# Last two expert pairs placed by matrix products instead of a scatter, with token rows loaded and added beside the last pair

## Chip, cores and metric

One of the eight cores of a Trainium2 chip runs the whole program in one launch. The metric is the device time of that program in microseconds (us); less is better. All data are 32-bit floats.

## What is computed

Two transformer blocks on 512 token rows of width 1024. The change touches the last stage only, a mixture of experts, and the normalisation behind it. Cut to what matters (NE = 32 experts, two of them chosen per token, hidden width 256):

```python
for e in range(N_EXPERTS):
    he = silu(xt @ w_gate[e]) * (xt @ w_up[e])
    y = y + combine[:, e:e + 1] * (he @ w_down[e])
x = x + y
out = rms_norm(x) * final_norm
```

`combine` is zero except for the two experts that the router chose for the token, and holds their weights there. So 1024 (token, expert) products have to be made, weighted, and added to 512 rows.

## The kernel before

The engines run five instruction streams written out by hand, tied by semaphores: TensorE (PE), VectorE (DVE), ScalarE (ACT), GpSimd (POOL) and SyncE (SP). Each stream is strictly in order, so a wait in one holds up all that stands behind it.

**The expert stage.** A tile holds 128 rows: 64 slots for one expert and 64 for another. 24 such tiles ("pairs", `NP = 24`) are worked through in a fixed order: 16 main pairs (experts 2m and 2m+1 for m = 0 to 15) and 8 for experts with more than 64 rows (`OVER_AT`). Pair 22 holds main pair 14 (experts 28 and 29), pair 23 main pair 15 (experts 30 and 31). For pair n:

- POOL gathers the token rows of the slots from DRAM by an indirect DMA (L741); slots with no token have an index out of bounds and move nothing.
- PE turns the tile (`turn_tile`, L2118 to L2124, 8 transposes into PSUM banks 4 and 5); DVE copies it out (`tile_turned`, L1585).
- PE makes gate and up (`gate_up`, L2126, L2134: 16 matmuls, two at a time on the two halves of the array's columns) into PSUM bank n % 2; ACT applies silu (`half_tile`, L1121), DVE multiplies (`product`, L1599).
- PE turns the hidden rows (`turn_hidden`, L2143), ACT copies them (`copies`, L1125), PE makes down (`down`, L2155) into PSUM banks 2 and 3.
- ACT copies bank 2 and DVE bank 3 to the row buffer YO[n % 3] (L1131, L1605), and POOL scatters the 128 rows to the DRAM array `pair_rows` (`y_d`, L745) at (choice, token).

PE takes the pairs so that its gate/up for n + 1 stands ahead of the hidden turn and down of n (L2162 to L2168). SP loads the expert weights (4 MB of gate and up, 2 MB of down for a main pair) as their buffers come free (L572 to L579); the weights of overflow pairs come by indirect DMA on POOL (L747 to L764).

**Routing** is computed ahead of the stage by DVE (L1508 to L1583): slot indices (SLOT, L1575), then the two weights of each token (WGT, L1579 to L1582); `v_wr` reaches 2 with the last of them. POOL starts the gathers at `v_sl` (L767); PE starts at the first gathered tile.

**The end of the kernel.** SP waits until PE has done all gate/up and until *all* 24 scatters have landed (L581 to L583), then loads the pair rows of the four token tiles, 8 loads of 512 KB (L587). DVE adds weight times row to X, 8 instructions (L1623). ACT sums squares (L1142), POOL makes the inverse root (L611, L613 through `root`), DVE scales by it and by the norm's weight (L1629, L1630), and ACT issues the four stores of 512 KB (L1145).

Of the kernel before, what the change touches and what calls it, by code (L numbers as in the profile page):

```python
# [159 lines left out]

def tile_order(i):

    return ORDER.get(i, tuple(range(TILES[i])))
# [9 lines left out]
def build(nc, a, out):  # L173
    with ExitStack() as ctx:
# [104 lines left out]
        YO = [RM[:, 4096:5120], RM[:, 5120:6144], WUKV[:, :]]  # L279
        HE = [RM[:, 6144 + 256 * n:6400 + 256 * n] for n in range(2)]  # L280
# [122 lines left out]

        d_g = [sem(f"pairs_loaded{t}") for t in range(4)]
# [84 lines left out]
        def _(sp):  # L489
# [102 lines left out]
        def _(g):  # L592
# [141 lines left out]

            wgr, wur, wdr = (a[f"w_expert_{s}_2"][0].rearrange("e (p k) c -> (e p) (k c)", p=P) for s in ("gate", "up", "down"))
# [7 lines left out]
            def scatter(n):  # L743
                rows = row_at(ap=SLOT[:, 24 + column(n):25 + column(n)], axis=0)
                g.indirect_dma_start(y_d, rows, YO[n % 3], None, bounds_check=TOPK * T_X - 1, oob_is_err=False).then_inc(m_st[n % 3], 16)  # L745

# [25 lines left out]
            gather(4)  # L772
            over_gate_up(3)
            for n in range(NP + 1):
# [17 lines left out]
        def _(act):  # L792
# [334 lines left out]
            def rows(n):  # L1127
                act.wait_ge(m_dn, 2 * n + 1)
                if n >= 3:
                    act.wait_ge(m_st[n % 3], 16 * (n // 3))  # L1130
                A(YO[n % 3][:, 0:512], PS[:, 2, :], ACT.Copy).then_inc(m_ya, 1)  # L1131

            half_tile(0)
            for n in range(NP):
                if n + 1 < NP:
                    half_tile(n + 1)
                copies(n)
                rows(n)

            for t in range(4):  # L1140
                act.wait_ge(v_g, 2 * t + 2)
                A(XN[:, t, :], X[:, 2 + t, :], ACT.Square, scale=D ** -0.5, accum_out=ss[:, t:t + 1]).then_inc(a_fm, 1)  # L1142
            for t in range(4):
                act.wait_ge(v_fn, t + 1)
                act.dma_start(out[0].rearrange("(t p) d -> p t d", p=P)[:, t, :], X[:, 2 + t, :]).then_inc(d_out, 16)  # L1145
# [3 lines left out]
        def _(v):  # L1149
# [432 lines left out]
            v.tensor_tensor(WGT[:, :, 1:2], WGT[:, :, 0:1], tiles(EXPS, [1, 1], off=10), ALU.mult).then_inc(v_wr, 1)  # L1582
# [18 lines left out]
            def down_rows(n):  # L1601
                v.wait_ge(m_dn, 2 * n + 2)
                if n >= 3:
                    v.wait_ge(m_st[n % 3], 16 * (n // 3))
# [3 lines left out]
            tile_turned(1)  # L1608
            product(0)
# [7 lines left out]
            j = 0  # L1617
            for t in range(4):
                v.wait_ge(d_g[t], 32)
                for k in range(2):  # L1620
                    if k == 1:
                        v.wait_ge(v_g, j)
                    v.scalar_tensor_tensor(X[:, 2 + t, :], YP[:, 2 * t + k, :], WGT[:, t, k:k + 1], X[:, 2 + t, :], ALU.mult,  # L1623
                                           ALU.add).then_inc(v_g, 1)
                    j += 1
            v.wait_ge(d_fw, 16)
            for t in range(4):
# [6 lines left out]
        def _(pe):  # L1634
# [481 lines left out]
            pe.wait_ge(v_sl, 1)  # L2116

# [8 lines left out]
            def gate_up(n):  # L2126
# [5 lines left out]
                for k in range(8):  # L2132
# [3 lines left out]
                last.then_inc(m_gu, 1)  # L2136
# [90 lines left out]
```

## Time and profile before

| | |
|---|---|
| median of 3 runs | 1624.77 us (1624.53 to 1625.59) |
| the profiled execution | 1624.51 us |
| its span | 1622.7 us (so 1.8 us lie outside the span) |
| PE busy | 1502.9 us, 93% of the span |
| DVE, ACT, POOL busy | 522.3, 449.6, 331.1 us |
| chain that ended last, by engine | PE 88%, DMA 3%, ACT 3%, DVE 3% |
| mean granted clock | 0.973 |

The busy shares say that PE is nearly always at work; the chain says that PE is also what the end of the kernel goes back to. But neither says anything of one stage, so the end of the kernel has to be read from its own rows: instructions in order of time, the chain's last pieces, and the packets of each DMA queue in short windows. A DMA queue's row gives the packets, the MB and the time its packets took as a share of 16 DMA engines in the window asked for.

### The profile page before, as it was taken

How to read it: one execution, taken by the hardware profiler on the slowest of the kernel's cores; microseconds unless marked ns; L12 is line 12 of the kernel's file. 1: busy time of each engine (PE TensorE's matmuls, PEld its weight loads, DVE VectorE, ACT ScalarE, POOL GpSimd, SP SyncE). 2: the span in 40 equal slices, each digit the busy share in tenths (PEclk: the TensorE clock that was granted, in tenths of full speed). 3: DMA queues.
4: the chain of work that ended last, by engine and by line, in shares of the span. 5: the costliest groups of instructions: out<-in, count | busy, mean ns of one | idle time of the engine just before them, and what ended most of it. 6: DMA issues, size and time to landing. Idle time of an engine off the chain costs nothing.

```text
span 1622.7 us, 17325 instructions
## 1 busy us (share of the span) xinstructions
PE 1502.9 (93%) x6765; PEld 785.3 (48%) x6765; DVE 522.3 (32%) x1124; ACT 449.6 (28%) x881; POOL 331.1 (20%) x357
## 2 busy tenths in 40 slices
PE   5998989999999989999999899999999499999992
PEld 2676544455675444455675444455455333333330
DVE  1073310656433210666432211122143412111214
ACT  2234322222763241233762110232232101101101
POOL 1010000453000110555000000004422134323312
PEclk9999999999999999999999999999999699999996
DMA  9654113230110212120100123110500779999994
GB/s 353 239 212 170 53 64 144 78 119 37 50 58 1 94 52 78 53 83 21 55 1 1 52 104 104 52 44 29 193 1 27 275 265 414 369 412 398 402 409 177
DMA packets 85128, 232.98 MB, mean 144 GB/s; under 512 B 17026, under 2 KB 24968, under 8 KB 70841
## 3 DMA queue, kind: packets, MB, share of 16 engines
q1 hardware_dynamic: 69426, 201.93, 33.0%
q0 software_dynamic: 13824, 24.16, 4.1%
q10 hardware_dynamic: 1798, 5.80, 0.9%
q8 instruction: 54, 0.88, 0.2%
q14 instruction: 26, 0.21, 0.0%
HBM read 266.42 MB, written 16.80 MB: 175 GB/s over the span
## 4 chain that ended last, share of the span: by engine, by line
PE 88%; DMA 3%; ACT 3%; DVE 3%; issue 2%; POOL 0%; SPq 0%; DVEq 0%; POOLq 0%; ACTq 0%
PE PS L1719 19%; PE PS L2134 10%; PE PS L1887 9%; PE PS L1950 7%; PE PS L2155 5%; PE PS L1799 5%; PE PS L1698 4%; PE PS L1948 3%; PE PS L2043 3%; PE PS L1821 3%; PE PS L1809 2%; PE PS L1761 2%; PE PS L1985 1%; DMA RING<-in_w_mod_dram 1%; PE PS L2012 1%
## 5 line engine op out<-in xcount | busy, mean ns | idle before, releaser
L1719 PE MATMUL PS<-RH,RING 128*128 128x512 f32 (+1 forms) x864 | 315.9, 522 | 2.2 <-DMA RING<-in_w_in_dram 2.2
L1719 PEld LDWEIGHTS PS<-RH,RING 128*128 128x128 f32 x864 | 162.4, 190 | 146.9 <-issue 136.1
L1887 PE MATMUL PS<-RING,RY 128*128 128x512 f32 x320 | 139.5, 593 | 0.0
L2134 PE MATMUL PS<-RING,RM 128*64 128x512 f32 x384 | 116.7, 609 | 8.4 <-issue 5.6
L611 POOL TENSOR_SCALAR SMALL<-SMALL 128x1 f32<-128x1 f32 (+1 forms) x36 | 11.0, 306 | 537.7 <-ACT WS L833 266.1
L1249 DVE SCALAR_TENSOR_TENSOR RM<-RM,COL 128x512 f32<-128x512 f32 (+1 forms) x180 | 115.1, 707 | 0.2
L1950 PE MATMUL PS<-RH,RING 128*128 128x512 f32 x256 | 113.8, 593 | 0.0
L1290 DVE TENSOR_REDUCE SMALL<-PS 128x1 f32<-128x768 f32 (+1 forms) x80 | 68.0, 850 | 136.7 <-PE PS L1799 136.7
L1799 PE MATMUL PS<-RK,RH 96*128 96x256 f32 (+1 forms) x288 | 105.9, 487 | 1.1 <-ACT WS L976 0.7
L1887 PEld LDWEIGHTS PS<-RING,RY 128*128 128x128 f32 x320 | 60.1, 190 | 72.7 <-issue 72.7
L613 POOL TENSOR_TENSOR SMALL<-SMALL 128x1 f32<-128x1 f32 (+2 forms) x58 | 61.6, 1062 | 87.4 <-DVE SMALL L1223 84.4
L2134 PEld LDWEIGHTS PS<-RING,RM 128*64 128x64 f32 x384 | 37.4, 140 | 83.5 <-issue 80.1
L1950 PEld LDWEIGHTS PS<-RH,RING 128*128 128x128 f32 x256 | 47.2, 190 | 55.0 <-issue 55.0
L1121 ACT ACTIVATE RM<-PS 128x256 f32<-128x256 f32 x24 | 9.2, 385 | 221.7 <-PE PS L2134 221.7
L1799 PEld LDWEIGHTS PS<-RK,RH 96*128 96x128 f32 x288 | 49.9, 191 | 41.3 <-issue 39.4
L1698 PE MATMUL PS<-RING,RH 128*128 128x416 f32 (+1 forms) x192 | 62.9, 488 | 4.4 <-ACT RH L845 4.4
L976 ACT ACTIVATE WS<-PS,SMALL 128x768 f32<-128x768 f32 (+1 forms) x80 | 64.9, 812 | 3.0 <-DVE SMALL L1290 2.9
L1809 PE MATMUL PS<-CST,WS 128*128 128x128 f32 x416 | 59.4, 274 | 6.5 <-ACT WS L967 3.5
L1599 DVE TENSOR_TENSOR RM<-RM,PS 128x256 f32<-128x256 f32 x24 | 10.1, 421 | 160.3 <-ACT RM L1121 160.3
L2134 PE MATMUL PS<-RK,RM 128*64 128x512 f32 x128 | 58.6, 612 | 0.0
L1809 PEld LDWEIGHTS PS<-CST,WS 128*128 128x128 f32 x416 | 49.3, 141 | 18.4 <-issue 12.0
L1948 PE MATMUL PS<-RING,RH 128*128 128x512 f32 x128 | 56.4, 596 | 0.0
(336 smaller groups left out, 2251.0 us busy)
## 6 DMA issues: line engine op xcount, KB each, us to landing
RING<-in_w_in_dram SPq DMA_DIRECT2D x18, 2048.0 KB, 8.6
RING<-in_w_mod_dram SPq DMA_DIRECT2D x12, 2048.0 KB, 9.2
RING<-in_w_expert_gate_dram SPq DMA_DIRECT2D x19, 1024.0 KB
RING<-in_w_expert_up_dram SPq DMA_DIRECT2D x19, 1024.0 KB
RING<-in_w_out_dram SPq DMA_DIRECT2D x8, 2048.0 KB, 8.2
RK<-in_w_expert_down_dram SPq DMA_DIRECT2D x8, 1024.0 KB
X<-in_w_expert_down_dram SPq DMA_DIRECT2D x8, 1024.0 KB
WS<-in_w_expert_down_dram SPq DMA_DIRECT2D x8, 1024.0 KB
```

Of the source, the lines that this page charges most:

```text
L976: A(PR[n % 2][:, 0:nk], src, ACT.Exp, bias=nmx[:, n % 4:n % 4 + 1], accum_out=DEN[:, q % 2, h:h + 1]).then_inc(a_e.sem, 1)
L1249: ins = v.scalar_tensor_tensor(acc, src, w, acc, ALU.mult, ALU.add)
L1290: v.tensor_reduce(nmx[:, n % 4:n % 4 + 1], free(PS[:, 2 * (n % 2), :], [1, nk]), AX, ALU.max, negate=True).then_inc(v_mx.sem, 1)
L1698: last = mm(o[:, 0:width], HT[:, k, t * P:(t + 1) * P], w[:, k, :], start=(k == 0), stop=(k == 7))
L1719: last = mm(o[:, 0:T], w[:, k, m * P:(m + 1) * P], HT[:, k, 0:T], start=(k == 0), stop=(k == 7))
L1799: last = mm(PS[:, 2 * (n % 2) + c0 // 512, 0:w], RHf[0:QK, h * 512 + q * P:h * 512 + (q + 1) * P], KT[0:QK, h, c0:c0 + w], start=True, sto ...
L1809: last = tr(PS[:, 4 + j // 4, (j % 4) * P:(j % 4 + 1) * P], PR[k % 2][:, j * P:(j + 1) * P], IDENT)
L1887: last = mm(PS[:, j % 2, :], YT[:, k, t * P:(t + 1) * P], w[:, k, :], start=(k == 0), stop=(k == 7))
L1948: last = mm(PS[:, w % 2, :], HT[:, k, tile], wt[:, k, :], start=(k == 0), stop=(k == 7))
L1950: last = mm(PS[:, w % 2, :], wt[:, k, tile], HT[:, k, :], start=(k == 0), stop=(k == 7))
L2134: last = mm(PS[64 * z:64 * z + 64, n % 2, :], XGT[n % 2][:, k, 64 * z:64 * z + 64], free(GU[n % 3][z], [2048, 2], [1, DE], off=DE * k), st ...
L2155: last = mm(PS[64 * z:64 * z + 64, 2 + c, :], HET[n % 2][:, j, 64 * z:64 * z + 64], DN[n % 2][z][:, 1024 * j + 512 * c:1024 * j + 512 * c ...
```

## The change

Pairs 22 and 23 are no longer scattered. Instead:

- **Routing.** Behind the weights, DVE builds for each of the two pairs a 128 x 512 matrix LAST[z] (token by slot, the token's weight where the slot holds it, else zero) with two multiplies and an add of 512 columns each, and three small operations. PE turns the two matrices (8 transposes) before the first tile, ACT copies them out (`LAST_T`). Slot indices of pairs 22 and 23 are clamped to 511, so that their gathers move all 128 rows.
- **Zero rows.** POOL clears YO[2] before the stage, and scatters it twice, to the places of pairs 22 and 23, behind gather 4.
- **PE's order at the end.** Gate/up of pair 23 is cut in two with hidden turn and down of pair 22 between; two placing products stand behind it, two ahead of down of pair 23, four behind it, and then eight for pair 23's rows. A placing product is 128 x 128 by 128 x 512; 16 of them fill the eight PSUM banks with the 512 x 1024 sums.
- **Pair rows beside the last pair.** SP now waits for the hidden product of pair 22 and for the scatters up to pair 21 only. DVE adds the pair rows of token tile 0 *ahead of* `product(23)`, tile 1 behind it, tiles 2 and 3 behind the copy of pair 23's rows.
- **Final stage.** DVE adds the placed rows from PSUM (1024 columns, one instruction a tile), and scaling by root and weight is one instruction instead of two; SP instead of ACT issues the stores.

```diff
+def stored(n, b):
+    return sum(k % 3 == b for k in range(min(n, NP - 2))) + (2 if b == 2 else 0)
+        LAST_T = [WPWf[:, 0:512], WUQf[:, 1024:1536]]
+        LAST, PART = [WS[:, 2048:2560], WS[:, 0:512]], WS[:, 2560:3072]
...
-            sp.wait_ge(m_gu, NP - 1)
+            sp.wait_ge(m_he, NP - 1)
             for b in range(3):
-                sp.wait_ge(m_st[b], 16 * (NP // 3))
+                sp.wait_ge(m_st[b], 16 * stored(NP - 1, b))
...
+            for t in range(4):
+                sp.wait_ge(v_fn, t + 1)
+                sp.dma_start(out[0].rearrange("(t p) d -> p t d", p=P)[:, t, :], X[:, 2 + t, :]).then_inc(d_out, 16)
...
+            g.wait_ge(p_pv2, 32)
+            link(g.memset(YO[2], 0.0))
...
+            def zero_last():
+                for n in (NP - 2, NP - 1):
+                    rows = row_at(ap=SLOT[:, 24 + column(n):25 + column(n)], axis=0)
+                    g.indirect_dma_start(y_d, rows, YO[2], None, ...).then_inc(m_st[2], 16)
...
             gather(4)
+            zero_last()
             over_gate_up(3)
-            for n in range(NP + 1):
+            for n in range(NP - 1):
...
+            act.wait_ge(p_la, 1)
+            for z in range(2):
+                last = A(LAST_T[z], PS[:, 6 + z, :], ACT.Copy)
+            last.then_inc(a_la, 1)
             half_tile(0)
             for n in range(NP):
-                if n + 1 < NP:
+                if n + 1 < NP - 1:
                     half_tile(n + 1)
                 copies(n)
                 rows(n)
+                if n == NP - 2:
+                    half_tile(NP - 1)
...
+            link(v.tensor_tensor(free(SCR, [4, 8], ...), free(ONEHOT, ...), free(FIRST, ...), ALU.mult))
+            link(v.tensor_tensor(free(SCR, [4, 8], ...), free(SCR, ...), free(WGT...), ALU.mult))
+            v.tensor_scalar(SLOT[:, 14:16], PS[:, 1, 270:272], float(NONE), float(T_X - 1), ALU.add, ALU.min)
+            for z in range(2):
+                for k, dst in enumerate((LAST[z], PART)):
+                    last = v.tensor_tensor(free(dst, [P, 4], [64, 2], [1, 64]), free(OHR, ...), free(SCR, ...), ALU.mult)
+                link(last)
+                last = v.tensor_tensor(LAST[z], LAST[z], PART, ALU.add)
...
+            last.then_inc(v_wr, 1)
             v.wait_ge(v_wr, 2)
...
             for n in range(NP):
-                if n + 1 < NP:
+                if n + 1 < NP - 1:
                     product(n + 1)
                 if n + 2 < NP:
                     tile_turned(n + 2)
+                if n == NP - 1:
+                    pair_sums(0)
+                    product(n)
+                    pair_sums(1)
                 down_rows(n)
...
+            pair_sums(2)
+            pair_sums(3)
+            last_sums(0)
+            last_sums(1)
             v.wait_ge(d_fw, 16)
-            for t in range(4):
-                v.wait_ge(g_fn, t + 1)
-                link(v.tensor_scalar(X[:, 2 + t, :], X[:, 2 + t, :], rs[:, t:t + 1], None, ALU.mult))
-                v.tensor_tensor(X[:, 2 + t, :], X[:, 2 + t, :], GB[:, :], ALU.mult).then_inc(v_fn, 1)
+            final_rows(0)
+            last_sums(2)
+            final_rows(1)
+            last_sums(3)
+            final_rows(2)
+            final_rows(3)
...
+            pe.wait_ge(v_wr, 2)
+            for z in range(2):
+                for t in range(4):
+                    last = tr(PS[:, 6 + z, t * P:(t + 1) * P], LAST[z][:, t * P:(t + 1) * P], IDENT)
+            last.then_inc(p_la, 1)
...
             def down(n):
...
+                if n == NP - 1:
+                    pe.wait_ge(a_la, 1)
+                    place(0, 3, 1)
+                    place(0, 0, 0)
...
+            def place(z, t, c):
+                return mm(PS[:, 2 * t + c, :], LAST_T[z][:, t * P:(t + 1) * P], YO[(NP - 2 + z) % 3][:, 512 * c:512 * c + 512],
+                          start=(z == 0), stop=(z == 1))
...
             for n in range(NP):
                 if n + 1 < NP:
-                    gate_up(n + 1)
+                    gate_up(n + 1, range(8) if n + 2 < NP else range(4))
                 turn_hidden(n)
                 if n + 2 < NP:
                     turn_tile(n + 2)
                 down(n)
+                if n + 2 == NP:
+                    gate_up(n + 1, range(4, 8))
+                    pe.wait_ge(m_ya, NP - 1)
+                    pe.wait_ge(m_yv, NP - 1)
+                    place(0, 2, 0)
+                    place(0, 2, 1)
+
+            pe.wait_ge(m_yv, NP)
+            place(0, 0, 1)
+            pe.wait_ge(m_ya, NP)
+            place(0, 1, 0)
+            place(0, 1, 1)
+            place(0, 3, 0)
+            for t in range(4):
+                place(1, t, 0)
+                place(1, t, 1).then_inc(p_fin, 1)
```

`pair_sums(t)` waits for the two loads of token tile t and runs the two weighted additions that stood at L1623; `last_sums(t)` waits for `p_fin` t + 1 and adds PSUM banks 2t and 2t + 1 to X; `final_rows(t)` waits for the root and does X times root times weight in one instruction.

## Rows read from the trace of the kernel before

**Rows 1.** The page: span, granted clock and DMA share in 40 slices.
```profile
span 1622.7 us, 17325 instructions
PEclk9999999999999999999999999999999699999996
DMA  9654113230110212120100123110500779999994
```

**Rows 2.** The chain that ended last, its last 47 us: start us, us, what.
```profile
1575.56 7.02 PE PS L2134 x32
...
1583.40 3.65 PE PS L2155 x16
1587.06 0.39 PE PS L2143 x2
...
1587.94 3.67 PE PS L2155 x16
...
1591.63 0.70 DVE WUKV L1605
...
1593.16 2.56 DMA pair_rows<-WUKV,SLOT
...
1595.81 0.33 SPq L587
...
1618.00 1.23 DVE X L1630
```

**Rows 3.** Groups by line and shape, 1575 to 1623 us: xcount | busy us, mean ns.
```profile
L1623 DVE SCALAR_TENSOR_TENSOR X<-RING,WGT,X 128x1024 f32<-128x1024 f32 x8 | 10.2, 1286 | 9.1 <-DMA RING<-pair_rows 8.9
...
L613 POOL TENSOR_TENSOR SMALL<-SMALL 128x1 f32<-128x1 f32 x4 | 5.6, 1390 | 0.3
L1630 DVE TENSOR_TENSOR X<-X,GB 128x1024 f32<-128x1024 f32 x4 | 4.9, 1226 | 0.1
...
L1142 ACT ACTIVATE RY<-X 128x1024 f32<-128x1024 f32 x4 | 4.2, 1058 | 17.6 <-DVE X L1623 17.6
...
L1142 ACT ACTIVATION_READ_ACCUMULATOR RY<-X 128x1 f32 x4 | 0.7, 186 | 0.0
```

**Rows 4.** Timeline: start us, us, engine, line, operation.
```profile
1199.06 3.60 PE L2043 MATMUL PS<-RING,WS 128*128 128x512 f32 x8
...
1571.19 0.42 DVE L1599 TENSOR_TENSOR RM<-RM,PS 128x256 f32<-128x256 f32 x1 [6.59 <-ACT RM L1121]
...
1577.13 0.98 POOL L745 DMA_INDIRECT pair_rows<-RM,SLOT x1 [10.72 <-DVE RM L1605]
...
1600.76 2.61 DVE L1623 SCALAR_TENSOR_TENSOR X<-RING,WGT,X 128x1024 f32<-128x1024 f32 x2 [8.44 <-DMA RING<-pair_rows]
```

**Rows 5.** DMA queues: 1577.1 to 1581, 1581 to 1586, 1588.5 to 1592.5, 1592.5 to 1596.1.
```profile
q1 hardware_dynamic: 197, 1.43, 94.8%
...
q0 software_dynamic: 144, 0.30, 15.5%
...
q0 software_dynamic: 144, 0.18, 12.1%
...
q0 software_dynamic: 144, 0.05, 5.0%
```

**Rows 6.** The chain around two restarts of PE at low clock.
```profile
1298.43 9.30 PE PS L2134 x32
...
1417.75 3.88 issue
1421.63 8.78 PE PS L2134 x32
```

**Rows 7.** Before the stage: a 512-column DVE operation, and the first gather on the chain.
```profile
1281.01 0.68 DVE L1558 TENSOR_TENSOR WS<-WS 128x512 f32<-128x512 f32 x1
...
1287.19 7.71 DMA RM<-normed_rows,SLOT
```

**Rows 8.** Window around gather 23: engines' busy us, clock, DMA share, GB/s.
```profile
1520.00:1530.00 10.00, 10.00 (x54) 3.88 (x52) 2.40 (x4) 1.34 (x3) 1.62 (x2) 1.00 0.97 369
```

More of the change, by code:

```diff
@@ L1581, in _ @@
             link(v.reciprocal(WGT[:, :, 0:1], total))
-            v.tensor_tensor(WGT[:, :, 1:2], WGT[:, :, 0:1], tiles(EXPS, [1, 1], off=10), ALU.mult).then_inc(v_wr, 1)
+            link(v.tensor_tensor(WGT[:, :, 1:2], WGT[:, :, 0:1], tiles(EXPS, [1, 1], off=10), ALU.mult))
+            link(v.tensor_tensor(free(SCR, [4, 8], [1, 4], off=16), free(ONEHOT, [32, 8], [1, 4], off=28), free(FIRST, [1, 8], [0, 4]), ALU.mult))
+            link(v.tensor_tensor(free(SCR, [4, 8], [1, 4], off=16), free(SCR, [4, 8], [1, 4], off=16),
+                                 free(WGT[:, :, :].rearrange("p t k -> p (t k)"), [1, 8], [0, 4]), ALU.mult))
+            v.tensor_scalar(SLOT[:, 14:16], PS[:, 1, 270:272], float(NONE), float(T_X - 1), ALU.add, ALU.min)
+            for z in range(2):
+                for k, dst in enumerate((LAST[z], PART)):
+                    last = v.tensor_tensor(free(dst, [P, 4], [64, 2], [1, 64]), free(OHR, [P, 4], [0, 2], [1, 64], off=64 * k),
+                                           free(SCR, [8, 4], [1, 2], [0, 64], off=16 + 4 * k + 2 * z), ALU.mult)
+                link(last)
+                last = v.tensor_tensor(LAST[z], LAST[z], PART, ALU.add)
+                if z == 0:
+                    link(last)
+            last.then_inc(v_wr, 1)
             v.wait_ge(v_wr, 2)
@@ L1608, in _, with pair_sums @@
             tile_turned(1)
+            def pair_sums(t):
+                v.wait_ge(d_g[t], 32)
+                xt = X[:, 2 + t, :]
+                for k in range(TOPK):
+                    link(v.scalar_tensor_tensor(xt, YP[:, 2 * t + k, :], WGT[:, t, k:k + 1], xt, ALU.mult, ALU.add))
             product(0)
             for n in range(NP):
-                if n + 1 < NP:
+                if n + 1 < NP - 1:
                     product(n + 1)
@@ L1614, in _, with last_sums, final_rows @@
                     tile_turned(n + 2)
+                if n == NP - 1:
+                    pair_sums(0)
+                    product(n)
+                    pair_sums(1)
                 down_rows(n)
[L1617 to L1625, printed above, removed]
-            v.wait_ge(d_fw, 16)
-            for t in range(4):
-                v.wait_ge(g_fn, t + 1)
-                link(v.tensor_scalar(X[:, 2 + t, :], X[:, 2 + t, :], rs[:, t:t + 1], None, ALU.mult))
-                v.tensor_tensor(X[:, 2 + t, :], X[:, 2 + t, :], GB[:, :], ALU.mult).then_inc(v_fn, 1)
+            def last_sums(t):
+                v.wait_ge(p_fin, t + 1)
+                v.tensor_tensor(X[:, 2 + t, :], X[:, 2 + t, :], free(PS[:, 2 * t, :], [1, D]), ALU.add).then_inc(v_g, 1)
+            def final_rows(t):
+                v.wait_ge(g_fn, t + 1)
+                v.scalar_tensor_tensor(X[:, 2 + t, :], X[:, 2 + t, :], rs[:, t:t + 1], GB[:, :], ALU.mult, ALU.mult).then_inc(v_fn, 1)
+            pair_sums(2)
+            pair_sums(3)
+            last_sums(0)
+            last_sums(1)
+            v.wait_ge(d_fw, 16)
+            final_rows(0)
[4 more added lines that the diff above has]
+            final_rows(3)
         @block.tensor
@@ L2124, in turn_tile, with gate_up @@
                 last.then_inc(m_xt, 1)
-            def gate_up(n):
+            def gate_up(n, ks=range(8)):
                 pe.wait_ge(m_xc, n + 1)
@@ L2131, in gate_up @@
                     pe.wait_ge(m_he, n - 1)
-                for k in range(8):
+                for k in ks:
                     for z in range(2):
@@ L2135, in gate_up @@
                                   free(GU[n % 3][z], [2048, 2], [1, DE], off=DE * k), start=(k == 0), stop=(k == 7))
-                last.then_inc(m_gu, 1)
+                if ks[-1] == 7:
+                    last.then_inc(m_gu, 1)
             def turn_hidden(n):
```

14 lines of the change are left out of this document (7 added, 7 removed).

## The prediction, made before the changed kernel was run

> **What bounds the kernel now.** I read the page first. PE works through nearly the whole span at the full clock, and the DMA engines stand at 0.9 or more through the second half of the expert stage [rows 1]. So two resources are near their limit there, and what lies behind the stage is neither. The chain's last pieces come next: gate/up of the last pair, two down products, DVE's copy, the last scatter, SP's loads, additions, final scaling [rows 2]. From the end of the last down (1587.94 + 3.67 = 1591.6) to the end of the span (1622.7) are 31.1 us with PE idle. Its price list: scatter 2.56; first load issued 1595.81, first addition 1600.76, so 4.95 to land a token tile's two loads [rows 2, 4]; eight additions of 1.29; the last DVE instruction ends at 1619.23, and 3.5 us of store and end follow [rows 2, 3]. The change takes the scatter, the loads and most additions out of these 31 us, and puts PE work in.
>
> **The loads' new start.** Loads now wait for scatter 21 only. It was issued at 1577.13 [rows 4], and it is tempting to let it land 2.56 us later, as the last one did. The queue rows say otherwise. From 1577.1 to 1581 only q1 (SP's weights) moved packets, 1.43 MB; all 144 packets of the scatter (q0) stand between 1581 and 1586 [rows 5]. The scatters of pairs 22 and 23, alone on the engines, were done inside the windows shown, some 2.5 us after their issue. So a scatter amid weight traffic took 8 to 9 us. What delays it, the down weights of pair 23 issued at about 1575.6, is still there. I take 1586.0 for SP's first load, 9.8 us earlier than before, and 1591.0 for tile 0's data.
>
> Here a rule speaks for the change. The Trainium skill (DMA: Bandwidth & Descriptors, Queues, rings and completion order) has each DMA engine alternate between the queues that have work, packet by packet; by that the scatter would share from its issue on and land near 1580 to 1582. The trace disagrees for the first 4 us after issue, in which q0 had no packet. What it would be worth is the third case below.
>
> **More bytes.** The clamped indices make gathers 22 and 23 move 256 rows. The two scatters moved 0.18 + 0.05 MB [rows 5], 56 rows of 4 KB, so 200 rows or 0.82 MB are new, 2.2 us at the 1.43 MB in 3.9 us of the full engines [rows 5]. They fall around 1514 to 1531, where the share dips to 0.97 for 10 us [rows 8]; the dip absorbs about half, and I push the queue's end, so the loads, by 1.1 us (bounds 0 and 2.2): data at 1592.1. Weights themselves have room: gate/up of pair 23 started right behind down, and of the 2.18 MB that q1 moved after 1577.1 some 2.1 are the down weights of pair 23 [rows 5], so those of pair 22 had landed by about 1577.3; they are now wanted at 1580.0, and 1.6 us are left.
>
> **PE up to the last product.** Half of pair 23's gate/up is 7.02 / 2 = 3.5, to 1579.1. Hidden turn to down is 1587.94 - 1587.06 = 0.88, now with nothing beside it; down 3.65, to 1583.6; second half, to 1587.1 [rows 2]. A placing product is a 128 x 128 by 128 x 512 float matmul; four such in L2043 (eight rows of the trace) took 3.60, so 0.9 each [rows 4]. Two of them: PE is free at 1588.9.
>
> **The new wait.** Behind DVE's copy of pair 22's rows stands `pair_sums(0)`, *ahead* of `product(23)`. It waits for tile 0's data at 1592.1 and takes 2.61 [rows 4]; only then comes the product, 0.42 [rows 4], at 1595.2 with the hops. Queued behind that product are PE's whole remaining work and DVE's copy of the last rows. Before, it ran right behind silu. PE idles from 1588.9 to 1595.2, 6.3 us, which nothing covers.
>
> **What PE does then.** Turn and copy 0.88, two placing products 1.8, down 3.67, DVE's copy 0.7 and hops: 1602.3. Four placing products 3.6, and two for tile 0 of pair 23: the first signal of placed rows at 1607.7; the others follow 1.8 apart, the last at 1613.1. `pair_sums(1)` fits beside PE (its data land 3 us behind tile 0's), tiles 2 and 3 (5.2 us) fit between 1602.3 and 1607.7.
>
> **The tail.** Addition from PSUM 1.29 (priced as an addition of 1024 columns in SBUF); ACT 1.06 + 0.19; POOL's root about 1.3 with DVE mostly idle (the power alone 1.39 on average beside busy DVE); `final_rows` 1.29 instead of two instructions [rows 3]. By DVE's order: sum 0, square, root, final 0, sum 2, final 1, sum 3 = 1.29 + 1.25 + 1.3 + 4 x 1.29 = 9.0, to 1616.7; then square, root 1.7 and final 3, 4.3, to 1621.0. PE's last signal (1613.1) comes before DVE asks for it at 1615.4. Plus 3.5: the span would be 1624.5.
>
> **PE's clock.** After the wait of 3.88 us at 1417.75 the next gate/up took 8.78 instead of 7.02, and after the start of the stage 9.30 [rows 6]: the granted clock was at its lower level, 1.2 of 2.4 GHz, for some us, and 1.8 to 2.3 us were lost. An idle time of 6.3 us should do the same. I take 2.3, lower bound 0; upper bound: everything left at the lower clock, which adds 11.3 before the first signal and makes the last one late by another 3.1, 14.4 in all.
>
> **Edits that cost nothing.** Routing: six 512-column operations of 0.68 [rows 7] and three small ones, 4.7 us from 1286.9; eight transposes at twice 0.39 for each two, 3.1; that ends at 1294.7, and the first gather lands only at 1287.19 + 7.71 = 1294.9 [rows 7]. The cover is thin; if it goes, up to 1 us is lost. Zero rows: two issues of 0.98 and 0.3 between them put pair 3's indirect weight loads 2.6 us back, wanted 30 us later; their bytes fall where the DMA's slice shows 0.7 [rows 1]. The clearing of YO[2], about 1 us on POOL, lies some 15 us before anything needs it. ACT's copies of LAST_T end before its first silu. SP's stores wait behind nothing.
>
> **The sum.** 1624.5 + 2.3 = 1626.8 us of span against 1622.7; with 1.8 outside the span **1628.6 us** against 1624.51 of the profiled execution and the median 1624.77: slower by 0.24%. In two terms: pair 23's down starts 9.9 us later than before (1597.8 against 1587.94), and from its end 23.0 us are left to go instead of 31.1, so 1.8 are lost at the full clock and 2.3 by the clock. About 0.2% (3.2 us) is what a measurement of this kernel can tell from no change.
>
> **Rivals.**
> - *The clock holds or the gathers' extra bytes are absorbed.* All as above without the 2.3, or also without the 1.1: 1626.3 or 1625.2, no difference that can be measured. For it: the clock's price rests on two restarts only. Against: 6.3 us is longer than the 3.88 us after which the clock did fall.
> - *The scatter lands early (the other side).* Mechanism: scatter 21 shares the engines from its issue and lands by 1580 to 1582; the loads then stand in q1 right behind the down weights, whose last 0.75 MB ran after 1581 [rows 5], so tile 0's 1.05 MB land near 1586.5 instead of 1592.1. `pair_sums(0)` ends at 1589.1, PE waits under 1 us, no clock is lost: 1628.6 - 5.6 - 2.3 = 1620.7, faster by 0.25%. It decides if the loads start before about 1582. This is the rule of the skill's DMA page put into this kernel; against it stand the q0 packets after 1581.
> - *The clock stays low to the end.* PE works in pieces of 2 to 4 us with waits of 0.5 to 0.8 between them; if that isn't enough to raise it, 1628.6 - 2.3 + 14.4 = 1640.7, slower by 1%. Against: at the start of the stage it rose within one gate/up.
> - *The stage itself stalls.* The saturated queue already lets PE wait 3.88 us at 1417.75 [rows 6]; if the new bytes or POOL's delay lengthen such a wait by 2 to 3 us, 1631.
>
> **How the numbers follow.** Forecast (the wait, with one stretch of low clock) 0.50; clock holds or bytes absorbed 0.22; early scatter 0.12; clock low for long 0.09; stage stalls 0.07. The prices of the forecast are good to about 2 us each way, and the bound to "slower" lies at 1628.0, so some six tenths of it (0.30) count as slower, with 0.16 of the last two: slower 0.46. Of the early scatter 0.09 is faster, with 0.01 from errors elsewhere: faster 0.10. Same 0.44. The range leaves out about a tenth on each side: the early scatter's better half below, the long low clock above: 1621.5 to 1633.
>
> **What would show it.** Right: SP's first L587 load at 1585 to 1588; DVE idle till 1590 to 1593 ahead of two additions that stand before the last product; PE idle 5 to 7 us before the last hidden turn; the granted clock at 0.5 for some us behind it; the six or so products behind the last copy 0.9 each; final instruction near 1623. Wrong: loads issued by 1582, PE waiting under 2 us, the clock at 1.00 throughout, POOL's roots well off 1.3 us, an addition from PSUM that takes far more than 1.3 us, or PE starting pair 0 later than 1295.

## The result: slower by 0.3%, and the profile after

The changed kernel took 1631.15 us (median of 5 runs, 1628.77 to 1632.8) against 1624.77 (median of 5, 1623.07 to 1626.88): ratio 1.0031, 95% interval 1.0019 to 1.0042. (The ratio is the one on record; the quotient of the two medians is a little larger, 1.0039.) The forecast was 1628.6 us, +0.24%. The profiled run took 1631.15 us too, with a span of 1629.3.

The page after, for [rows 1]. Slice for slice the granted clock and the DMA share are nearly those of before. What changed isn't to be seen at this scale, and the closer views are needed:

```profile
span 1629.3 us, 17422 instructions
...
PEclk8999999999999999999999999999999699999997
DMA  9655114231110212120100122110500779999993
```

Two points are needed before the traces can be compared. First, the part ahead of the expert stage moves by itself from run to run: the instruction that forms SLOT started at 1286.01 in the trace of before, at 1288.69 after, and at 1290.15 and 1288.80 in two further traces that differ from before only in their last microseconds. Second, the stage itself kept its length: from that instruction to the end of pair 21's down there were 289.55 us before (1286.01 to 1575.56), 288.84 after (1288.69 to 1577.53), and between 288.9 and 291.1 in the traces of the experiments. So I count everything from the end of pair 21's down, and call that point E. From E to the end of the span: 47.1 us before, 51.8 after. That is +4.7, against +5.0 by the ratio.

The chain that ended last, after (start us, us, what), for [rows 2]:

```profile
1573.92 3.61 PE PS L2218 x16
...
1579.08 8.22 DMA pair_rows<-RM,SLOT
...
1587.36 0.33 SPq L596
...
1587.73 4.56 DMA RING<-pair_rows
...
1592.31 1.30 DVE X L1651
...
1594.95 0.43 DVE RM L1637
...
1595.42 0.70 PE PS L2202 x2
...
1596.59 3.78 PE PS L2223 x4
1600.37 4.09 PE PS L2218 x16
...
1604.54 0.70 DVE WUKV L1643
...
1605.28 5.43 PE PS L2223 x12
...
1610.81 1.23 DVE X L1667
...
1620.31 0.22 POOL SMALL L623
...
1621.22 1.28 DVE X L1671
```

Read it downwards. The scatter of pair 21 is issued 1.5 us behind E, takes 8.22 us, the second load of token tile 0 another 4.6, and two additions later DVE comes to the last product (L1637). PE's last turn (L2202) waits for it. Then one pass of placing products, the last down, DVE's copy, the placing products of the first tile, and an alternation of DVE, ACT and POOL to 1622.50.

How long PE waited is in the timeline (start us, us, engine, line, operation, in brackets the idle time before and what ended it):

```profile
1595.42 0.69 PE L2202 MATMUL PS<-CST,RM 128*128 128x128 f32 x2 [3.39 <-DVE RM L1637]
```

What its clock did is in the windows of 2 us around it (length, then PE, PEld, DVE, ACT and POOL busy, granted clock, DMA share, GB/s):

```profile
1594.00:1596.00 2.00, 0.57 (x2) 0.29 (x2) 1.33 (x2) 0.00 (x0) 0.00 (x0) 0.62 1.03 401
1596.00:1598.00 2.00, 1.53 (x3) 0.84 (x3) 1.65 (x2) 0.38 (x1) 0.00 (x0) 0.50 1.02 416
1598.00:1600.00 2.00, 2.00 (x3) 0.34 (x1) 0.92 (x1) 0.00 (x0) 0.00 (x0) 0.50 0.82 332
1600.00:1602.00 2.00, 2.00 (x7) 0.63 (x8) 0.00 (x0) 0.00 (x0) 0.00 (x0) 0.67 0.03 10
1602.00:1604.00 2.00, 2.00 (x12) 0.56 (x8) 0.00 (x0) 0.60 (x1) 0.00 (x0) 1.00 0.00 0
```

PE idled 3.39 us, its clock fell towards the end of that time (0.62 in the window 1594 to 1596) to 0.50 (1.2 of 2.4 GHz), and was back at 1.00 from 1602. That is the forecast's mechanism, with a shorter wait.

The surprise stands at the other end. The last DVE instruction ended 43.7 us behind E before (1619.23) and 45.0 after (1622.50): only 1.3 later. But from there to the end of the span it took 3.5 us before and **6.8 after**. SP's waits at the program's closing line, after, show why (engine, line, waited for: total us, times, longest):

```profile
SPq L180 <- PEq L180: 4.0, 1, 4.0
SPq L180 <- DMA out_dram<-X: 2.3, 1, 2.3
```

The queue instructions of that closing line, after (duration in ns: shortest/median/longest, then first and last start):

```profile
L180 POOLq EVENT_SEMAPHORE  x2: 17/17/17, 1629.2 to 1629.2; - x2
...
L180 POOLq DRAIN  x1: 8542/8542/8542, 1620.6 to 1620.6; - x1
```

The last store had landed at 1625.2; then SP waited 4.0 us more. The view puts that wait down to PE's queue, but PE's drain had ended long before (it began at 1608.0 and took 7.9). What ends at 1629.2 is POOL's closing DRAIN: 1620.6 + 8.54. POOL's last instruction, the power of the last root, ended at 1621.2, so the drain ends 8.0 us behind it. The same lines of the kernel before:

```profile
L174 POOLq EVENT_SEMAPHORE  x2: 17/17/17, 1622.5 to 1622.6; - x2
...
L174 POOLq DRAIN  x1: 8897/8897/8897, 1613.6 to 1613.6; - x1
...
L174 SPq COMPARE_BRANCH  x1: 38/38/38, 1621.9 to 1621.9; - x1
```

There too the span ended with POOL's drain (1613.6 + 8.9 = 1622.5, 8.0 behind the last root's end at 1614.54), but the stores had landed only 0.6 us earlier, so it passed for "store and end". Which engine issues the stores makes no difference here: ACT before, SP after, and the last store has landed 2.7 us behind the last DVE instruction in both (1619.23 to 1621.9, 1622.50 to 1625.2). The change moves the last root from 39.0 to 43.7 us behind E (1614.54 and 1621.19), and the end of the span follows it.

### The profile page after: what moved, and what is told of

Read it like the earlier page. It is cut to its first block, busy times and chain, and to the rows that moved or that the text cites. A ratio compares the mean times of both kernels' runs of the same rounds, so it can differ in the third digit from the quotient of the medians.

```text
span 1629.3 us, 17422 instructions
## 1 busy us (share of the span) xinstructions
PE 1526.4 (94%) x6805; PEld 795.8 (49%) x6805; DVE 528.8 (32%) x1133; ACT 450.6 (28%) x883; POOL 328.9 (20%) x358
## 4 chain that ended last, share of the span: by engine, by line
PE 89%; DMA 3%; ACT 3%; DVE 3%; issue 2%; POOL 0%; SPq 0%; POOLq 0%; DVEq 0%; ACTq 0%
PE PS L1772 19%; PE PS L2192 10%; PE PS L1940 8%; PE PS L2003 7%; PE PS L2218 5%; PE PS L1852 5%; PE PS L1751 4%; PE PS L2001 3%; PE PS L2096 3%; PE PS L1874 3%; PE PS L1862 3%; PE PS L1814 2%; PE PS L2038 1%; PE PS L2065 1%; PE PS L2181 1%
## 5 line engine op out<-in xcount | busy, mean ns | idle before, releaser
L625 POOL TENSOR_TENSOR SMALL<-SMALL 128x1 f32<-128x1 f32 (+2 forms) x58 | 58.3, 1005 | 87.3 <-DVE SMALL L1247 84.4
L1637 DVE TENSOR_TENSOR RM<-RM,PS 128x256 f32<-128x256 f32 x24 | 10.1, 421 | 153.6 <-ACT RM L1142 153.6
L2192 PE MATMUL PS<-RH,RM 128*64 128x512 f32 x128 | 56.4, 592 | 0.6 <-issue 0.6
```

The lines of the kernel that those rows point to most:

```text
L625: g.tensor_tensor(dst, src, HALF[:, 0:w], ALU.pow).then_inc(done, 1)
L2192: last = mm(PS[64 * z:64 * z + 64, n % 2, :], XGT[n % 2][:, k, 64 * z:64 * z + 64], free(GU[n % 3][z], [2048, 2], [1, DE], off=DE * k), st ...
```

## The experiments

Two theories were to be told apart. **The wait:** the loss comes from `pair_sums(0)` ahead of `product(23)`, through PE's idle time and its clock. **The end:** the span ends with POOL's drain, so the place of the last root counts. Rivals were the extra bytes of the gathers and the traffic around the scatter. For each run the table gives the ratio to the kernel before, as it ran in the same session as the experiment (medians 1625.75 to 1626.46 us there; the quotient of two medians can lie up to 0.0008 off the ratio), and from its trace the last DVE instruction's end behind E, the time from there to the end of the span, and both together. The times behind E are of one trace each; the kernel before and e10 and e3, which differ from it only behind the last scatter, have 43.7, 44.4 and 44.5 in the first column of times.

| kernel | ratio (95%) | last DVE behind E | to the end | sum |
|---|---|---|---|---|
| before | 1 | 43.7 | 3.5 | 47.1 |
| changed | 1.0031 (1.0019 to 1.0042) | 45.0 | 6.8 | 51.8 |
| e1 product first | 0.9996 (0.9986 to 1.0006) | 38.7 | 6.9 | 45.5 |
| e5 three extra products | 1.0022 (1.0014 to 1.0031) | 46.5 | 6.9 | 53.4 |
| e11 five extra products | 1.0015 (1.0006 to 1.0024) | 42.8 | 6.9 | 49.7 |
| e3 before, late POOL | 1.0041 (1.0027 to 1.0056) | 44.5 | 8.4 | 52.8 |
| e2 roots by Ln, Exp | 1.0045 (1.0029 to 1.0061) | 51.6 | 3.0 | 54.6 |
| e7 roots by Sqrt | 1.0000 (0.9990 to 1.0010) | 44.8 | 3.0 | 47.9 |
| e10 before, roots by Sqrt | 1.0002 (0.9993 to 1.0011) | 44.4 | 3.2 | 47.6 |
| e6 sums first | 1.0022 (1.0011 to 1.0033) | 45.4 | 6.9 | 52.3 |
| e4 no clamp | 1.0028 (1.0017 to 1.0039) | 45.8 | 6.8 | 52.6 |
| e8 down weights later | 1.0011 (1.0002 to 1.0019) | 43.2 | 6.8 | 50.0 |
| e9 = e1 + e7 | 0.9957 (0.9944 to 0.9971) | 38.7 | 3.1 | 41.8 |
| e12 = e1 + e7 + e8 | 0.9980 (0.9970 to 0.9991) | 41.9 | 3.0 | 44.9 |

### The wait and the clock

**e1**, the changed kernel with one line moved:

```diff
                 if n == NP - 1:
-                    pair_sums(0)
                     product(n)
+                    pair_sums(0)
                     pair_sums(1)
```

> The changed kernel with product(23) ahead of pair_sums(0) on DVE, nothing else. Theory (the new wait costs, by idle time and by low clock): in the changed kernel's trace PE was free at 1592.0 and got the product at 1595.4, then ran the turn, two placing products and down at 8.6 us instead of 5.9. With the product right behind silu PE has no idle time there and stays at the full clock, so the span falls by 3.4 + 2.7 = about 6 us, to about 1623 (device about 1625, level with the kernel before). Rival (the loads' additions only fill time that DVE would need anyway, so the work moves behind the last copy): DVE then has 5.2 us of additions between down and the placed rows, and the gain is 1 us or less.

Ratio 0.9996 and 45.5 us behind E: 6.3 less than the changed kernel (by the two ratios 5.7). The chain of e1 (start us, us, what) holds neither the scatter nor a load; up to the last down it is PE with ACT's short copies between:

```profile
1591.81 1.92 PE PS L2223 x4
1593.72 0.23 PE PS L2202 x2
...
1594.41 1.98 PE PS L2223 x4
1596.40 3.61 PE PS L2218 x16
```

PE goes from the placing products into the last turn without a gap. From the start of the turn to the end of down are 6.29 us, against 9.04 in the changed kernel (1595.42 to 1604.46). So of the 6.3 us, 2.7 are low clock and the remaining 3.6 are about the idle time of 3.39. The idle time is the larger part of what this order loses.

**e5** and **e11** keep the wait and try to take only the clock's part away, with products whose result is not used (in e11 the range is 5):

```diff
             def turn_hidden(n):
+                if n == NP - 1:
+                    pe.wait_ge(a_la, 1)
+                    for _ in range(3):
+                        mm(PS[:, 7, :], LAST_T[0][:, 0:P], YO[(NP - 2) % 3][:, 0:512], start=True, stop=True)
                 pe.wait_ge(m_he, n + 1)
```

> The changed kernel with three products of 128x128 by 128x512 put ahead of PE's wait for the last product; their result goes to PSUM bank 7 and is overwritten, so they add no value and take 2.6 us of the 3.4 us in which PE idles. Theory (the idle time lowers the clock, and that costs 2.7 us of its own: turn 0.70 instead of 0.39, two placing products 3.78 instead of 1.9, down 4.09 instead of 3.6): the clock stays at 1.00, the time from the start of the last hidden turn to the end of down falls from 9.0 to about 6.4 us, and the span from gate/up's end on by about 2.7. Rival (only the wait costs; the clock is made up for by DVE's additions behind it): the pieces shrink but the end moves less than 0.5 us.

e5 didn't settle it. In its trace tile 0's data came late (first addition at 1594.29, 7.0 us behind the first load instead of 5.0), three products (2.7 us) ended before that, PE was idle another 3.5 us ahead of its last turn at 1597.40, and the clock fell to 0.50 again (from 1599): turn to the end of down 8.2 us. The edit hadn't produced the condition that it was to test. Hence e11:

> As the run with three products in PE's wait, but five (4.3 us), since with three PE still idled 3.2 us (tile 0's rows came later in that run) and the clock fell to 0.5 all the same. Theory (low clock costs 2.7 us of its own): now PE doesn't idle, the clock stays at 1.00, the last turn starts at most 1 us later than the product allows, and turn to end of down takes 6.4 us instead of 9.0; in all 1.5 to 2.5 us less than the changed kernel behind the last product. Rival (the slow pieces have another reason than the idle time): they stay at 9.0.

Its chain (start us, us, what) shows the turn at once behind the product, and the work behind it at full speed; its windows read 1.00 in every stretch of 2 us from 1590 to 1602:

```profile
1594.20 0.45 PE PS L2206 x2
...
1595.11 1.98 PE PS L2227 x4
1597.09 3.61 PE PS L2222 x16
```

Turn to the end of down took 6.50 instead of 9.04, the wait for the product being unchanged. The clock's price is 2.5 us here. At the end of the span 2.1 us of it are left (51.8 to 49.7); by the ratios it is 1.0031 to 1.0015, some 2.6 us, with overlapping intervals.

### What ends the span

**e3** tests the drain on the kernel before, where nothing else moves:

```diff
                 root(rs[:, t:t + 1], ss[:, t:t + 1], g_fn)
+            g.wait_ge(v_fn, 4)
+            g.tensor_tensor(nmx[:, 0:1], HALF[:, 0:1], HALF[:, 0:1], ALU.mult)
```

> The kernel before with one tiny POOL multiply (128x1) that waits for the last rows of DVE (1619.2 in its trace). Theory (the end is POOL's last instruction plus 8.0 us): the span ends at about 1619.3 + 0.3 + 8.0 = 1627.6 instead of 1622.7, 5 us later. Rival (stores end the span): no change, since the multiply ends before the last store has landed.

One multiplication of 128 x 1 on POOL, of which nothing uses the result, made the kernel before 0.41% slower, 6.7 us. SP's wait at the closing line, in e3:

```profile
SPq L174 <- PEq L174: 5.6, 1, 5.6
```

And POOL's instruction of that line, in e3 (ns, first and last start):

```profile
L174 POOLq DRAIN  x1: 8145/8145/8145, 1623.6 to 1623.6; - x1
```

POOL's last instruction ended at 1623.8, the drain at 1631.75, the span at 1631.9. Again 8.0 us.

**e2** takes the last roots off POOL, to ACT:

```diff
-            for t in range(4):
-                g.wait_ge(a_fm, t + 1)
-                root(rs[:, t:t + 1], ss[:, t:t + 1], g_fn)
...
+            A(nmx[:, 0:1], epsc, ACT.Ln)
             for t in range(4):
                 act.wait_ge(v_g, t + 1)
-                A(XN[:, t, :], X[:, 2 + t, :], ACT.Square, scale=D ** -0.5, accum_out=ss[:, t:t + 1]).then_inc(a_fm, 1)
+                link(A(XN[:, t, :], X[:, 2 + t, :], ACT.Square, scale=D ** -0.5, accum_out=ss[:, t:t + 1]))
+                link(A(ss[:, t:t + 1], ss[:, t:t + 1], ACT.Ln, bias=epsc))
+                A(rs[:, t:t + 1], ss[:, t:t + 1], ACT.Exp, scale=-0.5).then_inc(g_fn, 1)
```

> The changed kernel with the four last inverse roots made by ACT (logarithm and exponential, about 0.6 us a root instead of 0.9 on POOL), so that POOL's last instruction is scatter 21. Theory (the end of the span is POOL's last instruction plus about 8.0 us, which its closing drain takes; the stores land 4 us before that in the changed kernel): without late POOL work the span ends at the landing of the last store plus under 1 us, some 3.5 us earlier, about 1625.5. Rival (stores end the span, as the prediction had it): no change, or 0.3 us each for the quicker roots, at most 1 us in all.

Half of it came: 3.0 us from the last DVE instruction to the end, so the drain is out of the way. But the last DVE instruction came 6.6 us later, so its trace ends 2.8 us later than the changed kernel's (54.6 behind E). The ratio, 1.0045, is higher too, with overlapping intervals. ACT's timeline gives the reason; its end, for the last tile:

```profile
1627.16 1.28 ACT L1168 ACT_TABLE_LOAD   x1
1628.45 0.29 ACT L1168 ACTIVATE SMALL<-SMALL 128x1 f32<-128x1 f32 x1
1628.77 1.28 ACT L1169 ACT_TABLE_LOAD   x1
1630.06 0.20 ACT L1169 ACTIVATE SMALL<-SMALL 128x1 f32<-128x1 f32 x1
```

Ln and Exp in turn each load a table of functions here, so a root costs 3.1 us. My edit carried a cost of its own. The Trainium skill (ScalarE: Activation LUTs, What ACT_TABLE_LOAD costs) gives about 1283 ns for a load, which the trace confirms at 1.28, and a drain of about 1380 ns more for every switch of set; of that the trace shows nothing, the loads stand directly between their neighbours.

**e7** avoids that: Square and Sqrt on ACT, the reciprocal on DVE (the removal on POOL as in e2):

```diff
+            A(nmx[:, 0:1], epsc, ACT.Sqrt)
             for t in range(4):
                 act.wait_ge(v_g, t + 1)
-                A(XN[:, t, :], X[:, 2 + t, :], ACT.Square, scale=D ** -0.5, accum_out=ss[:, t:t + 1]).then_inc(a_fm, 1)
+                link(A(XN[:, t, :], X[:, 2 + t, :], ACT.Square, scale=D ** -0.5, accum_out=ss[:, t:t + 1]))
+                A(ss[:, t:t + 1], ss[:, t:t + 1], ACT.Sqrt, bias=epsc).then_inc(g_fn, 1)
...
                 v.wait_ge(g_fn, t + 1)
+                link(v.reciprocal(rs[:, t:t + 1], ss[:, t:t + 1]))
```

> The changed kernel with the four last roots as a square root on ACT and a reciprocal on DVE, POOL with nothing behind scatter 21. In the run with logarithm and exponential each root loaded two function tables of 1.28 us, which ate the gain, but POOL's drain ended 40 us before the span. Theory: with one table the root takes about 0.3 us on ACT and 0.2 on DVE, nothing of POOL is late, and the span ends under 1 us behind the last store: 3.5 to 4.5 us earlier than the changed kernel. Rival (what ended the span there was something else that POOL only happened to cover): less than 1 us.

The closing line of e7, POOL's drain and SP's first instruction behind the stores (ns, first and last start):

```profile
L180 POOLq DRAIN  x1: 12851/12851/12851, 1579.9 to 1579.9; - x1
...
L180 SPq COMPARE_BRANCH  x1: 38/38/38, 1626.0 to 1626.0; - x1
```

The last DVE instruction ended 44.8 us behind E instead of 45.0, practically where it was, and the end came 3.0 us behind it instead of 6.8. POOL's drain now runs from 1579.9, beside the stage's end, and the span ends with the last store (1626.0). What differs is where and how the root is made, and DVE's own end hardly moved by it, so the 3.8 us between 6.8 and 3.0 are what the drain costs the changed kernel. **e10** puts the same roots into the kernel before:

> The kernel before with the same square-root form of the last roots, POOL with nothing behind its last scatter. Theory: there the drain ended only 0.6 us behind the last store's landing, so the gain is 0.5 to 1 us. Rival (POOL's roots cost the kernel before as much as the changed one): 4 us.

1.0002, no difference. That fits the 0.6 us by which the drain ended behind the stores in before, and shows that e7's gain isn't one of cheaper roots: before had next to nothing there to win, the changed kernel has.

**e6** tries to bring the last root forward by order alone, with `last_sums(2)` and `last_sums(3)` ahead of all `final_rows`:

```diff
             last_sums(1)
+            last_sums(2)
+            last_sums(3)
             v.wait_ge(d_fw, 16)
             final_rows(0)
-            last_sums(2)
             final_rows(1)
-            last_sums(3)
             final_rows(2)
```

> The changed kernel with all four last_sums ahead of the four final_rows on DVE. It brings the last square and POOL's last root forward (PE's last placed rows are there 2 us before DVE asks for them) while the last store stays where it is. Theory (POOL's last root plus 8.0 us ends the span): 1.5 to 2 us earlier than the changed kernel from the last placed rows on. Rival (the last store ends it): no change, 0.3 us at most.

No gain to be told (1.0022, 52.3 us). From the first addition from PSUM to the last square it took 6.3 us (1610.17 to 1616.51) instead of 8.3 (1610.81 to 1619.07), but the last root ran beside three `final_rows` on DVE. POOL's timeline, third and fourth root of e6:

```profile
1616.03 0.22 POOL L623 TENSOR_SCALAR SMALL<-SMALL 128x1 f32<-128x1 f32 x1 [0.84 <-ACT RY L1169]
1616.34 0.57 POOL L625 TENSOR_TENSOR SMALL<-SMALL 128x1 f32<-128x1 f32 x1
...
1617.74 1.20 POOL L623 TENSOR_SCALAR SMALL<-SMALL 128x1 f32<-128x1 f32 x1 [0.84 <-ACT RY L1169]
1619.03 1.46 POOL L625 TENSOR_TENSOR SMALL<-SMALL 128x1 f32<-128x1 f32 x1
```

0.79 us of work against 2.66, for the same two instructions. The Trainium skill (SBUF — State Buffer, Who interferes with whom) states that a DVE instruction with two inputs from SBUF contends with a POOL instruction that reads SBUF, for a shared pair of ports that is an exclusive lock. The trace agrees: `final_rows` has X and GB as such inputs, and beside it the times are stretched; beside the additions that read one input from PSUM the first three roots kept 0.22 and 0.57. What the order gives, the slow root takes back. So the run doesn't test an earlier root; its drain, too, ended 8.0 us behind the last root's end (1620.49 and 1628.4).

### The bytes and the scatter

**e4** leaves out the clamp of the indices of the last two gathers, so that their unused rows are not loaded:

```diff
-            v.tensor_scalar(SLOT[:, 14:16], PS[:, 1, 270:272], float(NONE), float(T_X - 1), ALU.add, ALU.min)
```

> The changed kernel without the clamp of slot indices 14 and 15, so gathers 22 and 23 move 56 rows instead of 256 (slots without a token keep older rows, whose weight in LAST is zero). Theory (the 0.82 MB push the queue's end by about 1.1 us): gate/up of pair 23 starts without the 0.6 us of waiting that the changed kernel shows, scatter 21 and so SP's loads come about 1 us earlier after gate/up of pair 23 has started, and the span shrinks by 1 us. Rival (the DMA's free time before 1531 takes the bytes): no difference.

The bytes are really gone: in the window 1530 to 1540 the DMA engines moved 345 GB/s at a share of 0.92, against 414 at 1.03 after, some 0.7 MB. The time is not: 1.0028, and the scatter landed 9.39 us behind its issue. The forecast's 1.1 us for the extra bytes isn't confirmed by anything.

**e8** holds the down weights of pair 23 (2.1 MB) back on SP until tile 0's two loads are issued:

```diff
             sp.wait_ge(m_dn, 2 * (NP - 2))
-            load_down(NP - 1)
...
                     sp.dma_start(YP[:, 2 * t + k, :], pairs[:, k, t, :]).then_inc(d_g[t], 16)
+                if t == 0:
+                    load_down(NP - 1)
```

> The changed kernel with the loads of pair 23's down weights behind the loads of token tile 0 on SP instead of ahead of the wait for scatter 21. Theory (the scatter is late because q1 holds 2.1 MB of weights issued 1.5 us before it): with only the rest of pair 22's weights in q1 the scatter lands 3 to 5 us after its issue instead of 8.2, tile 0's rows are there before 1588 on the changed kernel's clock, DVE adds them while PE is still at gate/up, PE's wait of 3.4 us and the low clock are gone, and the span falls by about 6 us, as with the product put first. Down weights of pair 23 still land before they are wanted. Rival (a scatter amid the stage takes some 8 us whatever q1 holds): landing after 8 us again, no gain.

Its chain (start us, us, what; the long "issue" is PE waiting for the down weights: its down product waits for nothing else that isn't long done):

```profile
1579.13 5.54 DMA pair_rows<-RM,SLOT
...
1585.17 4.46 DMA RING<-pair_rows
...
1593.64 1.98 issue
1595.62 3.52 PE PS L2223 x4
```

The scatter landed in 5.54 us instead of 8.22: against 8.1 to 9.4 in the traces with the weights in place, so they did delay it, by some 2.7. The DMA queues show where: in the changed kernel no packet of the scatter (q0) stands before 1583.0, 3.9 us behind its issue, while q1 held the engines at a share of 0.91 and then 1.01; in e8 the first ones stand 1.4 to 1.9 us behind the issue (66 of 144 between 1580.5 and 1581). But the weights are needed too: PE now waited 1.98 us for them ahead of its placing products, at low clock. The net was 1.8 us less than the changed kernel in the trace. The 5.54 are still twice the 2.56 of a scatter alone [rows 2], and not by a late start: alone, too, the first packets stood 1.4 to 1.8 us behind the issue (1593.16, and 123 of 144 between 1594.6 and 1595). What took longer is the spread of the packets, down to the last 8, which moved one by one between 1583 and 1584.7. Why was not tried.

### The best of them

**e9** is e1 and e7 together.

> The changed kernel with both mends: product(23) ahead of pair_sums(0), and the four last roots by a square root on ACT and a reciprocal on DVE. Theory (the two losses stand one behind the other: 6 us of wait and clock, 4 us of POOL's drain): 10 us less than the changed kernel, about 1620, so 0.3 to 0.4% faster than the kernel before. Rival (with the wait gone, DVE's own additions bind the tail, and quicker roots give little): 1624, level.

1620.84 us (median of 5 runs, 1619.1 to 1622.42) against 1626.46 for the kernel before in the same session, ratio 0.9957 (0.9944 to 0.9971): faster than both kernels. The parts add up: 6.3 by e1 and 3.9 by e7 make 10.2, and e9 is 10.0 us below the changed kernel (51.8 to 41.8). Its chain (start us, us, what):

```profile
1579.33 8.46 DMA pair_rows<-RM,SLOT
...
1590.43 9.79 DMA RING<-pair_rows
...
1600.24 1.30 DVE X L1650
...
1615.24 1.28 DVE X L1671
```

Now PE is off the chain: the last tile's loads land at 1600.22 and four additions follow. **e12** adds e8's later weights, to bring those loads forward:

> Product first, square-root roots, and the down weights of pair 23 behind the loads of tile 0. The down weights moved back made PE wait 2.0 us for them ahead of the last down, though the scatter landed 5.5 instead of 8.2 us after its issue. Theory (with the product first the rows' landing is no longer on the chain, so an early scatter gives nothing and late down weights cost their wait): 1 to 3 us slower than product first with square roots alone. Rival (tile 0's additions done earlier shorten DVE's tail): 1 us faster than that.

It was slower than e9 (0.9980 against 0.9957, the intervals just touching; 44.9 against 41.8 us behind E), though its scatter had landed within 5.0 us: PE reached the last down earlier than in e8 and waited for its weights. The piece of its chain ahead of the placing products:

```profile
1592.25 2.34 issue
```

With nothing else to wait for, holding back the weights costs more than the earlier scatter gives.

## Why the prediction came out as it did

Slower by about 0.2% was forecast and 0.3% measured. That the total fits so well is luck: two errors of some 3 us stood against each other, an end that was 3.3 us longer than forecast and a way there that was 2.8 us shorter. Behind E the forecast had 51.2 us (1626.8 - 1575.56), and 51.8 were measured.

**The step that failed** is "Plus 3.5: the span would be 1624.5", resting on "3.5 us of store and end follow". It was read as a fixed cost behind the last DVE instruction. e3 and e7 show that it was nothing fixed: in before as in after, the span ends with POOL's drain, 8.0 us behind POOL's last instruction. Before, POOL was done 4.7 us ahead of DVE (1614.54 and 1619.23), and the drain ended at nearly the same time as the stores. In the changed kernel `last_sums(3)` is followed only by square, root and one `final_rows`, so POOL ends 1.3 us ahead of DVE. The end took 6.8 us: 3.3 more than forecast. No rival had it. The trace of before had it to read: POOL's DRAIN at the program's last line ends with the span, while the chain of waits, as it ends with the last busy instruction, doesn't show it.

**The mechanism of the wait** held, with other sizes: `pair_sums(0)` ahead of the last product, PE idle, low clock, recovered within one down. e1 undoes it and gains 6.3 us. Its sizes, on the way to the first placed signal (33.2 us behind E; forecast 1607.7 - 1575.56 + 2.3 = 34.4):

- SP's first load 9.8 us behind E, forecast 11.5, of which 1.1 was the push by more bytes. Without that term 10.4 is left, close. The scatter took 8.22 us; by the forecast 8.9 without the push.
- From the first load to the first addition 4.95, forecast 4.95.
- PE was free at 14.5 instead of 13.3: it waited 0.54 for the weights of gate/up 23, and turn to down took 1.37 instead of 0.88. The "1.6 us left" for the down weights of pair 22 weren't there: behind ACT's copy PE waited another 0.5 us with nothing but them outstanding. e4, without the extra bytes, had no wait ahead of that gate/up; but a trace of the kernel before (e3) had 0.3 there, so the bytes as its cause aren't shown.
- So the idle time was 3.4 us, not 6.3. The data came 1.7 us sooner and PE 1.2 later.
- The clock cost 2.7 us (e1) or 2.5 (e11), forecast 2.3. The rival in which it holds fell: 3.4 us of idle time were enough, less than the 3.88 of [rows 6].
- A placing product took 0.9 at full clock (x12 records, six products, in 5.43), as forecast.

**The tail** took 11.8 us from the first signal to the last DVE instruction's end instead of 13.3. The additions from PSUM took 1.22 (forecast 1.29). The root took 0.9 in both places where it counted, forecast 1.3 and 1.7: the power at 1.39 in [rows 3] had been a mean beside a DVE busy with operands from SBUF, and here DVE stood idle (0.57).

**The other rivals.** The early scatter didn't happen: 8.22 us here, 8.1 to 9.4 in the other traces with the weights in place. This is where the Trainium skill (DMA: Bandwidth & Descriptors, Queues, rings and completion order) has the queues alternate packet by packet. For the first 3.9 us behind the issue the trace doesn't show that, q1 alone moved packets; from 1583 to 1585 both queues did (73 of q1, 83 of q0). e8 shows that the traffic accounts for 2.7 of the 8.22 us. A clock that stays low to the end: no, 1.00 from 1602. A stage that stalls: no, 288.8 us against 289.6. Routing cost nothing: from the SLOT instruction to the first gate/up 12.33 us after (1288.69 to 1301.02), 12.42 before (1286.01 to 1298.43); PE had turned the two matrices by 1296.30 and waited another 1.3 us for the first gather, so the thin cover held.

**The account** from 47.1 to 51.8 us behind E: +3.3 by the drain, +1.3 before it. In that 1.3 stand the wait and the clock, 6.3 together by e1; without them the change would have brought DVE's end 5.0 us forward (43.7 to 38.7). With neither wait nor late root it is 0.43% faster than the kernel before, as e9 shows. The idea of the change is sound, and its two losses lie in one line of DVE's order and in the engine that computes four numbers per partition.

What stays open: why a scatter with only little traffic beside it still takes 5.0 to 5.5 us, and whether a third pair placed by products would free the loads still sooner; neither was tried.

## What to carry to other kernels

Ask what ends the span, not only what ends the chain of waits: look at each engine's closing DRAIN, and keep POOL's last instruction some 5 us ahead of the last DVE instruction (the drain's 8.0 us less the 3.0 that the stores and the end take here), or give it to another engine. When work that waits for a transfer is slotted in beside a late stage, put it behind the instruction that feeds the busiest engine, not ahead of it; the order within one queue was worth 6.3 us here, 2.7 of them through the clock. And check a forecast term by term even when its total fits.

## What the runs showed of the hardware that I had not expected

- POOL's closing drain ends 8.0 us behind POOL's last compute instruction: 1614.5 to 1622.5, 1621.2 to 1629.2, 1623.8 to 1631.75. Where POOL's last work was the scatter, the drain ended 7.9 us (e10) to 11.7 us (e7) behind the end of its issue. A single 128 x 1 multiplication placed at the end made a 1625 us kernel 0.41% slower.
- On ACT, Ln and Exp in turn load a table of 1.28 us each time, two for a root, which I hadn't foreseen; Square and Sqrt in turn loaded none between the tiles (square 1.06, root 0.30).
- The same two POOL instructions of 128 x 1 took 0.22 + 0.57 with DVE idle or adding from PSUM, and 1.20 + 1.46 beside DVE's 128 x 1024 operations from SBUF.
- A small scatter (0.3 MB) amid weight traffic took 8.1 to 9.4 us, 5.0 to 5.5 with 2.1 MB of that traffic held back; alone, with 0.05 MB, 2.56. Its first packet came 3.9 us behind the issue in the first case and some 1.4 to 1.9 in the others.
- The start of the expert stage moved by up to 4.1 us between traces (1286.01 to 1290.15) with the code ahead of it unchanged. An effect of 2 us is read from a fixed point near it, not from the ends of the spans.
